# Fused two-model block on one core: attention fills of the second block reordered, and its weighted values moved to the other PSUM ring

## The reference

```python
xn = rmsnorm(x, norm_mix)
(u_rnn, u_gate, q, k_c, v_c, k_s, v_s, k_w, v_w, g_nsa, g_a, g_b) = split(xn @ w_in)
h_a = rg_lru(causal_depthwise_conv(u_rnn, conv_w, conv_b), gate_a, gate_x, lru_lambda)
y_a = h_a * gelu(u_gate, approximate=True)          # width 1344
y_b = nsa_mixer(q, k_c, v_c, k_s, v_s, k_w, v_w, g_nsa, ...)
merged = sigmoid(g_a) * (y_a @ proj_a) + sigmoid(g_b) * (y_b @ proj_b)
h = x + merged @ w_out
return h + square(relu(rmsnorm(h, norm_mlp) @ w_mlp_in)) @ w_mlp_out
```

## Time and profile before

| | us |
|---|---|
| median of 3 runs | 1670.17 (1668.87 to 1675.4) |
| profiled execution | 1670.89 |
| its span, first to last instruction | 1669.1 |
| mean granted TensorE clock | 0.966 |
| VectorE busy | 1029.2 (62%) |
| ScalarE busy | 800.5 (48%) |
| POOL busy | 241.7 (14%) |

### The profile page before, as it was taken

How to read it: one execution, slowest core, us unless ns; L and a number is a source line. 1 busy time by engine, 2 the same in 40 slices (tenths; PEclk the granted TensorE clock), 3 DMA queues, 4 the chain that set the end, 5 groups by cost and what they waited for, 6 DMA issues and landing times.

```text
span 1669.1 us, 25362 instructions
## 1 busy us (share of the span) xinstructions
PE 1562.8 (94%) x10403; PEld 1407.2 (84%) x10403; DVE 1029.2 (62%) x1704; ACT 800.5 (48%) x1435; POOL 241.7 (14%) x225
## 2 busy tenths in 40 slices
PE   9969999899998999998989999799988799989999
PEld 6859988799986789987889987587976699979987
DVE  5735476668755575468578865446654486646643
ACT  4525453356642446444446652353445564435532
POOL 2400032131101230032031111003010041100000
PEclk9979999989999999999999999799999899989999
DMA  8763254345565534245245555355311244625553
GB/s 318 241 112 127 90 189 177 126 152 180 186 219 176 177 112 142 89 164 203 102 167 187 177 195 196 126 188 183 102 54 48 76 141 147 211 101 185 190 181 126
DMA packets 41027, 261.33 MB, mean 157 GB/s; under 512 B 4512, under 2 KB 5152, under 8 KB 14672
## 3 DMA queue, kind: packets, MB, share of 16 engines
q1 hardware_dynamic: 35600, 238.44, 41.5%
q0 software_dynamic: 2944, 15.69, 3.8%
q10 hardware_dynamic: 2368, 5.58, 0.9%
HBM read 254.98 MB, written 4.19 MB: 155 GB/s over the span
## 4 chain that ended last, share of the span: by engine, by line
PE 74%; DVE 12%; ACT 5%; DMA 4%; issue 3%; POOL 2%; ACTq 0%; DVEq 0%; POOLq 0%; SPq 0%
PE ps L478 66%; PE ps L581 3%; DVE lows L1499 2%; DMA d_scr<-PT 2%; POOL sm L2184 2%; PE ps L667 1%; ACT wh L998 1%; DMA raw<-d_wst 1%; ACT S L1411 1%; DVE ar L2002 1%; DVE sm L1532 1%; DVE xs L1529 1%; PE ps L688 1%; DVE S L2064 1%; PE ps L577 1%
## 5 line engine op out<-in xcount | busy, mean ns | idle before, releaser
L1499 DVE TENSOR_TENSOR lows<-raw,wh 128x1024 fp32r<-128x1024 f32 (+3 forms) x473 | 546.1, 1174 | 247.3 <-ACT wh L998 244.3
L478 PE MATMUL ps<-xTr,wh 128*128 128x256 f32 (+2 forms) x3664 | 673.4, 287 | 10.6 <-DVE xTr L1518 6.3
L478 PEld LDWEIGHTS ps<-xTr,wh 128*128 128x128 f32 (+2 forms) x3664 | 574.8, 193 | 15.2 <-issue 7.1
L998 ACT CAST wh<-raw 128x1024 fp32r<-128x1024 f32 (+3 forms) x473 | 455.5, 989 | 161.4 <-DMA raw<-d_wst 142.6
L478 PE MATMUL ps<-xTr,lows 128*128 128x256 f32 (+2 forms) x1832 | 522.5, 285 | 0.0
L478 PEld LDWEIGHTS ps<-xTr,lows 128*128 128x128 f32 (+2 forms) x1832 | 352.5, 192 | 0.0
L478 PE MATMUL ps<-wh,arR 128*128 128x512 f32 x928 | 296.4, 398 | 3.5 <-DVE ar L1652 3.5
L478 PEld LDWEIGHTS ps<-wh,arR 128*128 128x128 f32 x928 | 175.3, 189 | 47.4 <-DVE ar L1652 5.3
L478 PE MATMUL ps<-lows,arR 128*128 128x512 f32 x464 | 184.2, 397 | 0.0
L478 PE MATMUL ps<-arR,wh 128*128 128x256 f32 (+1 forms) x832 | 149.0, 282 | 2.2 <-DVE lows L1499 2.2
L478 PE MATMUL ps<-wh,xTr 128*128 128x512 f32 x384 | 125.4, 406 | 11.6 <-DVE xTr L1518 6.7
(11 more groups left out here) (265 smaller groups left out, 1564.2 us busy)
## 6 DMA issues: line engine op xcount, KB each, us to landing
raw<-d_wst SPq DMA_DIRECT2D x196, 1024.0 KB, 4.8
raw<-d_wst SPq DMA_DIRECT2D x24, 512.0 KB, 3.5
raw<-d_wst SPq DMA_DIRECT2D x12, 896.0 KB, 4.5
raw<-d_wst SPq DMA_DIRECT2D x8, 672.0 KB, 4.7
ar<-d_lnp POOLq DMA_DIRECT2D x5, 1024.0 KB, 5.1
raw<-d_wst SPq DMA_DIRECT2D x8, 441.0 KB, 3.6
d_scr<-PT POOLq DMA_DIRECT2D x1, 3072.0 KB, 35.3
ar<-d_par POOLq DMA_DIRECT2D x2, 1192.0 KB, 9.6
```

What stands on the lines that cost most here:

```text
L478: op = e.matmul(out, s, m, start=start and i == 0, stop=stop and i == len(pairs) - 1)
L998: e.copy(high_of(m), raw_of(m)).then_inc(*high.done(m))
L1499: e.tensor_tensor(low_of(m), raw_of(m), high_of(m).bitcast(F32), ALU.subtract).then_inc(*low.done(m))
```

## The change

Three of the four `ug` products in front of the attention, 9, 10 and 11, become filling steps. The list is dealt out anew: three `conv`, then for each lru block and each third of it one dense step (`conv` 3 to 11, then `ug` 9 to 11) and two `lru` steps, and the three `decay` at the end: 42 steps in all. And the weighted values `pv2` take their bank from M in place of A.

```diff
-        lru_steps = [("conv", n) for n in range(RN)]
-        lru_steps += [("lru", n, wi, jt) for n in range(4) for wi in range(2) for jt in range(3)]
+        dense_steps = [("conv", n) for n in range(RN)] + [("ug", n) for n in range(9, RN)]
+        lru_steps = dense_steps[:3]
+        for n in range(4):
+            steps = [("lru", n, wi, jt) for wi in range(2) for jt in range(3)]
+            for k in range(3):
+                lru_steps += [dense_steps[3 + 3 * n + k], *steps[2 * k:2 * k + 2]]
         lru_steps += [("decay", 9 + k) for k in range(3)]
...
# tensor
-            for n in range(8, 12):
-                gelu_gate(n)
+            gelu_gate(8)
...
                     kind, m, *how = next(lru_todo, ("none", 0))
+                    if kind == "ug":
+                        gelu_gate(m)
...
-                    b = A.take(w, ("pv2", i, un), vec, "o2", i, un)
+                    b = M.take(w, ("pv2", i, un), vec, "o2", i, un)
...
# scalar: the same two edits as in tensor for gelu_gate
# vector
-            for n in range(8, 12):
-                lows_for("ug", n)
+            lows_for("ug", 8)
...
+                    if kind == "ug":
+                        lows_for("ug", m)
...
-                                    A["pv2", i, un][:, 0:256].rearrange("p (h d) -> p h d", d=64),
+                                    M["pv2", i, un][:, 0:256].rearrange("p (h d) -> p h d", d=64),
```

## The result

The changed kernel takes 1677.86 us (median of 10 runs) against 1669.66 for the kernel before in the same session (10 runs). The ratio of the two is 1.0039, 95% interval 1.0029 to 1.0049: slower by 6.5 us, inside the 0.5% that the prediction called no change (the two medians are 8.2 us apart; I go by the ratio). The forecast was +1.5 us. One of the ten runs took 1668.57 us at a granted clock of 0.968, the other nine 1675.18 to 1680.26 us at 0.959 to 0.965. The profiled execution spans 1675.1 us against 1669.1.

A forecast was written before the change was run, and what follows sets the result against it. VectorE was taken to bound both attention halves. Terms -8.4 - 2.0 + 3.4 + 7.0 + 1.5 sum to +1.5 us on the median 1670.17, so 1671.7 us, range 1658 to 1681.

The forecast's parts named there:

- Ahead of the attention, -8.4: Before the attention: without ug 9, 10 and 11 TensorE arrives 8.4 us earlier and finds its inputs ready.
- First half, -2.0: Second block's attention, queries 0 to 127: VectorE's work plus a fetch wait sums to 60.2 against 62.2 us.
- Second half, +3.4: Second block's attention, second half: fewer decays and bank waits, more convolutions, lows, late fetches and loads; net +3.4 us.
- The ring: Second half: with the new bank VectorE's 0.75 us wait for the second transpose goes in six units, counted 4.5 us.
- The fetches: Second half: weight fetches for conv 11 and g2 0 come late again, costing 3.2 us.
- The loads: Second half: three gelus among exps make six table loads, 7.7 us of ScalarE, mostly hidden; charged 1.0 us.
- Tail, +7.0: Between attention and sqrt: three more decays cost 6.5 us and an eviction 0.5.
- Restart, +1.5: Behind the sqrt: TensorE idles about 7 us before g2 3 and the clock falls; charged 1.5 us, bounds 0 and 3.5.
- TensorE becomes the bound: Rival, attention: new work falls into VectorE's waits, halves near 52.5 and 69 us, total 1653.8 us; chance 0.15.
- Late fetches and loads fully covered: Milder rival, attention: late fetches and table loads cost nothing, -5.7 - 1.0, 1665 us; chance 0.13.
- Ring stays: Rival, second half: the second transpose finds another late holder, the 4.5 us stay, 1676 us; chance 0.09.
- bare loads: Slower rival, attention: six table loads lie bare on the chain, 7.7 in place of 1.0 us, 1678.4 us; chance 0.13.

The follow-up runs named there:

- The fastest kernel: Changed kernel with casts called at most two groups ahead, three filling steps in four units, VectorE's second decay instruction behind the next unit's maxima: 0.9935 of before (1660.17 us).
- the kernel with late casts: Changed kernel with the planner calling a piece's cast at most two groups ahead instead of three: 0.9979 of before.
- the amended kernel: Changed kernel with casts at most two groups ahead and three filling steps instead of two in four units: 0.9955 of before (1663.06 us) without the decay deferral.
- the other: Kernel before with pv2's bank in M and VectorE's second decay instruction issued behind the next unit's maxima: 0.9944 of before (1662.3 us).

## Why the prediction was right, and where its terms were not

The forecast held (1671.7 in a range of 1658 to 1681; +1.5 us against +6.5 measured), and so did its mechanism: the work taken out ahead of the attention comes back in it and as a bare tail. The signs came too: the three casts that wait for a DMA are those named (conv 8, conv 11, g2 0), five decays are left in the second half and four behind it, six loads are new, TensorE idles 7.68 us ahead of g2 3. The sqrt comes 11.6 us after dense work resumes (1336.20), not some 15. Of "units of 7 to 9 us" four of seven held (7.96 to 8.85 us), three took 9.56, 10.39 and 9.59. The sum is 4.5 us short of the span's +6.0: the three stretches up to the second half's end and the tail were all put too low, by 1.4 to 1.9 us each, and the start and the restart too high, by 1.0 and 1.1. By its steps:

- **Ahead of the attention, -8.4.** The first of the query and key transposes came 9.4 us earlier, 0.96 of it present already before the gelus (1160.69 against 1159.73). Right.
- **First half, -2.0.** 65.1 became 64.5: -0.5. The count of VectorE's work was good, the fetch wait in it was not: I gave it 2.5 us, and taking it away gave 4.5. The cast waited 4.19 us, nearly the whole fetch of the earlier trace rows: SyncE started the fetch at 1215.12 and ScalarE stood from 1215.50 on. I had taken off what VectorE still had to do, but it is ScalarE that waits.
- **Between the halves, 0.** It grew from 9.2 to 11.0 us, and I had named no term for it. What differs is the clock. In the kernel before it was granted at its upper level all through; in the changed kernel it fell to the lower one (half, 1.2 for 2.4 GHz) for 6.8 us of this stretch. TensorE has no idle time left there, and its 16 compressed score products take 2.98 us in place of 1.89. First the kernel before, then the changed one:

```profile
1252.37:1261.57 9.20, 7.86 (x49) 6.52 (x51) 3.98 (x11) 4.18 (x9) 0.00 (x0) 1.00 0.14 41
1253.27 1.89 PE L895 MATMUL ps<-ar 128*128 128x60 f32 x16
...
1242.44:1253.39 10.95, 10.95 (x48) 9.06 (x49) 2.89 (x9) 4.18 (x9) 0.00 (x0) 0.69 0.08 11
1243.34 2.98 PE L900 MATMUL ps<-ar 128*128 128x60 f32 x16
```

  It is so in all fourteen kernels of the table: where this stretch takes 8.7 to 9.2 us the clock in it is 1.00, where it takes 11.0 to 12.6 us it is 0.59 to 0.69. Ahead of the fall TensorE had stood 4.14 us (until 1233.70, for exponentials) and 2.86 us (until 1242.44, for POOL). The kernel with the bank in A also stood 2.86 us there and kept the full clock; its low stretch had come earlier, from 1229.1 to 1235.9. So the moved steps change when the clock falls; which of them does it stays open, since no run was made for it.
- **Second half, +3.4.** 74.2 became 79.0: +4.8. Errors inside partly cancel. The ring was put at -4.5 by VectorE's wait for the second transpose, and is worth -6.3 in this stretch; TensorE's own 9.4 us in the earlier trace rows was the nearer row. (With the new dealing it is worth 6.4 there, 85.4 against 79.0, and 5 us by the ratios.) The fetches were put at 3.2 and removal gave 4.8. The loads, at 1.0, cost about 0.5. With these the sum would be +2.7; 2.1 us of the stretch stay unassigned. TensorE's work was put at about 63 us and is 69.65, some 15 of it at the lower clock.
- **Tail, +7.0.** From the outputs' transposes to sqrt 6.5 became 15.4 us, +8.9: three further decays and the eviction as reckoned (7.0), 1.28 for the sixth load, which the sum had among the hidden ones, and 0.6 for ScalarE's wait on the last lru product. The idle of about 7 us before g2 3 was 7.68.
- **Restart, +1.5.** It is what is left of the span's +6.0 = -9.4 - 0.5 + 1.8 + 4.8 + 8.9 + 0.4, so at most 0.4 behind the sqrt. The clock did fall behind the idle: from 1349.8 to 1356.5 it was granted at 0.50. But the clock cost more where no term had it, between the halves.

The term that was most mis-sized is the fetch: 5.7 us in the sum, 9.3 us when taken away in both halves. On the table loads the prediction weighed the Trainium skill, page "ScalarE: Activation LUTs", section "What ACT_TABLE_LOAD costs" (2.66 us for a switch, 1.38 of it a drain) against the earlier trace rows, and the rows hold: from the load at 1298.23 to the activation at 1299.53 it is 1.30 us.

```profile
1298.23 1.28 ACT L1316 ACT_TABLE_LOAD   x1
...
1299.53 0.38 ACT L1316 ACTIVATE ar<-ps 112x256 f32<-112x256 f32 x1
...
1300.40 1.28 ACT L1417 ACT_TABLE_LOAD   x1
...
1302.16 0.51 ACT L1417 ACTIVATE S<-S,sm 128x256 f32<-128x256 f32 x1 [0.48 <-DVE sm L2074]
```

The second of the two is covered altogether: it is over at 1301.68, and ScalarE still waits 0.48 us for the maxima.

Of the rivals, "TensorE becomes the bound" fell by its times: neither half came near the 52.5 and 69 us that it asks for (64.5 and 79.0), and the busy share of the first half went down. In the second half it was half true: TensorE is busy 88% of it and idle only 9.35 us. The fastest kernel still has TensorE idle 9.7 of 70 us in its second half (60.31 busy). "Late fetches and loads fully covered" is, as to the fetches, what the kernel with late casts shows, and it gained more than the 6.7 us written down for both. "Ring stays" and "bare loads" did not come. The advice of that page of the Trainium skill to batch calls by set stands in its section "Table sets: the hidden batching unit"; here six loads against it cost about 2 us by the runs.

## What to carry to other kernels

A change that deals work evenly moves it against a prefetch that is counted in steps. Before dealing, ask of each piece which earlier use frees its buffer and how long before the cast that is; here taking that away gave back 10 us, where 11 to 14 had been lost. What the units have no room for comes out bare behind them, in front of the one instruction (sqrt) that everything later queues behind, and moving a single cast past it shifts the idle by one product only. In an in-order queue take away the wait that ends last: taking the first one (the reciprocal's) made the kernel 6 us slower, taking the second (the decay's) made it 2.9 us faster in the amended kernel and shortened the second half from 67.9 to 63.6 us in the other. And read the granted clock of every stretch that grows for no reason you can name: between the halves the whole difference went with it.

## What had not been expected of the hardware

Tanh ran under the gelu's table: at 1336.96 in the changed kernel it follows a gelu with no load between, and the exp behind it loads for 1.28 us at 1337.57, so the place of the load differs from where the function changes. Whether a function needs a load so depends on what ran before it: behind a unit's exponentials the same tanh (1296.54) has none ahead of it either.
